# Conv-GLU layer on one core: eight Strassen pairs at distance two in the second half of the down projection, and a home of their own for the weights' sums

## What is computed

```python
def conv_glu_ffn(u, w_up, conv_ffn, b_conv_ffn, w_down):
    h = causal_dwconv(u @ w_up, conv_ffn) + b_conv_ffn
    return (jax.nn.silu(h[..., :D_FF]) * h[..., D_FF:]) @ w_down
...
        x = x + conv_glu_ffn(rms_norm(x, g_ffn[l]), w_up[l], conv_ffn[l], b_conv_ffn[l], w_down[l])
```

## Time and profile before

| | |
|---|---|
| time, median of 3 runs | 1744.62 us (1741.98 to 1744.79) |
| the profiled execution | 1744.25 us, its span 1742.5 us |
| busy: PE, DVE, ACT | 1732.3, 1184.1, 956.1 us (99, 68, 55%) |
| granted TensorE clock, mean | 0.999 |
| weights loaded by SP | 600 issues of 512 KB, median 3.3 us from issue to landing |

### The profile page before, as it was taken

One profiled execution on the slowest core, in us unless ns is written; L12 is line 12 of the kernel. 1 busy time (PEld: TensorE's weight loads), 2 busy tenths in 40 slices (PEclk: granted clock), 3 DMA queues, 4 the chain that ended last, 5 costly groups with the idle time before them and its releaser, 6 DMA issues.

```text
span 1742.5 us, 25685 instructions
## 1 busy us (share of the span) xinstructions
PE 1732.3 (99%) x8706; PEld 1470.0 (84%) x8706; DVE 1184.1 (68%) x1618; ACT 956.1 (55%) x1271; POOL 9.9 (1%) x22
## 2 busy tenths in 40 slices
PE   9999999999999999999999999999999999999999
PEld 7888888888788888888888888888888888888887
DVE  6788876667755455545565667777777666788777
ACT  7765656666754444444664565555555555555453
POOL 0000000000000000000000000000000000000000
PEclk9999999999999999999999999999999999999999
DMA  8555554476655555556855445555555555555654
GB/s 321 192 172 172 171 173 158 169 166 166 163 188 191 189 192 192 187 195 221 301 183 189 147 169 193 187 189 190 187 188 191 193 188 186 169 206 192 206 194 169
DMA packets 90960, 330.93 MB, mean 190 GB/s; under 512 B 10224, under 2 KB 10480, under 8 KB 89872
## 3 DMA queue, kind: packets, MB, share of 16 engines
q1 hardware_dynamic: 89424, 321.96, 54.7%
q0 software_dynamic: 1472, 8.12, 2.8%
HBM read 326.83 MB, written 2.10 MB: 189 GB/s over the span
## 4 chain that ended last, share of the span: by engine, by line
PE 93%; DVE 2%; DMA 2%; ACT 2%; issue 1%; SPq 0%; ACTq 0%; DVEq 0%
PE ps L381 22%; PE ps L362 13%; PE ps L364 13%; PE ps L363 13%; PE ps L384 11%; PE ps L756 4%; PE ps L758 4%; PE ps L757 4%; DMA w_raw<-in_stream 2%; PE ps L484 1%; PE ps L485 1%; PE ps L483 1%; PE ps L528 1%; PE ps L527 1%; ACT w_hi L843 1%
## 5 line engine op out<-in xcount | busy, mean ns | idle before, releaser
L1397 DVE TENSOR_TENSOR w_lo<-w_raw,w_hi 128x1024 fp32r<-128x1024 f32 x514 | 626.8, 1224 | 459.1 <-ACT w_hi L843 458.6
L843 ACT ACTIVATE w_hi<-w_raw 128x1024 fp32r<-128x1024 f32 x514 | 539.7, 1057 | 507.8 <-PE ps L364 309.7
L381 PE MATMUL ps<-u,w_hi 128*128 128x512 f32 x1664 | 580.8, 395 | 0.0
L384 PE MATMUL ps<-u,w_lo 128*128 128x256 f32 x1664 | 461.8, 278 | 0.0
L381 PEld LDWEIGHTS ps<-u,w_hi 128*128 128x128 f32 x1664 | 312.1, 188 | 72.4
L384 PEld LDWEIGHTS ps<-u,w_lo 128*128 128x128 f32 x1664 | 312.4, 188 | 0.2
L362 PE MATMUL ps<-w_hi,u 128*128 128x512 f32 x608 | 241.0, 396 | 0.6 <-DVE w_lo L1429 0.6
L364 PE MATMUL ps<-w_hi,u 128*128 128x512 f32 x608 | 237.4, 390 | 0.0
L363 PE MATMUL ps<-w_lo,u 128*128 128x512 f32 x608 | 237.0, 390 | 0.0
L362 PEld LDWEIGHTS ps<-w_hi,u 128*128 128x128 f32 x608 | 114.4, 188 | 24.6 <-issue 1.0
L364 PEld LDWEIGHTS ps<-w_hi,u 128*128 128x128 f32 x608 | 114.3, 188 | 24.2
(11 more groups left out here) (404 smaller groups left out, 2373.2 us busy)
## 6 DMA issues: line engine op xcount, KB each, us to landing
w_raw<-in_stream SPq DMA_DIRECT2D x600, 512.0 KB, 3.3
x_tok<-in_x SPq DMA_DIRECT2D x2, 1024.0 KB, 8.6
mem_raw<-in_mem_by_feature POOLq DMA_DIRECT2D x2, 1024.0 KB, 7.3
x_tok<-in_x POOLq DMA_DIRECT2D x2, 1024.0 KB, 7.6
mem_tok<-in_mem POOLq DMA_DIRECT2D x2, 1024.0 KB, 14.7
x_t<-in_x_t SPq DMA_DIRECT2D x7, 256.0 KB, 5.2
w_raw<-in_stream SPq DMA_DIRECT2D x4, 256.0 KB, 5.1
m_st<-ncm POOLq DMA_DIRECT2D x8, 128.0 KB, 9.4
```

Source lines behind the costliest of these rows:

```text
L381: pe.matmul(ps[:, bank + m, :], w_hi[:, s, lo:lo + P], act[:, kc, :, :].rearrange("p h t -> p (h t)"), start=(kc == 0), stop=False)
L384: mm = pe.matmul(ps[:, bank + m, T:2 * T], w_lo[:, s, lo:lo + P], act[:, kc, 0, :], start=False, stop=(kc == KC - 1))
L843: act.activation(w_hi[:, s, :], w_raw[:, s, :], ACT.Copy).then_inc(hi_made, 1)
L1397: TTo(w_lo[:, s, :], w_raw[:, s, :], w_hi[:, s, :].bitcast(F32), ALU.subtract).then_inc(lo_made, 1)
```

## The change

The second pass gets eight fast pairs at positions 4, 6, ..., 18, a distance of two; the first keeps its six. The activations' sums are made for eight pairs, in iterations 2 to 9 of the up projection. `u_sum` gets a place of its own, so that only `u_hi` and `u_lo` wait for `fast_done`. In the loop over n the staging comes ahead of the split and one pair earlier (n + 3); pair 2 is staged before the last iteration of the up projection, which is written out instead of looped. The last steps of iteration 10 are put after the splits of pairs 2, 3, 5 and 6. The space comes from the scratch of software DMAs, 4096 instead of the default.

```diff
-FAST_AT = (4, 7, 10, 13, 16, 19)
+FAST_AT = ((4, 7, 10, 13, 16, 19), (4, 6, 8, 10, 12, 14, 16, 18))
...
+ORDER = [_order(at) for at in FAST_AT]
+FAST = [(j, p, ORDER[j][p] // 2 - 1) for j in range(2) for p in FAST_AT[j]]
...
+        u_sum = sb("u_sum", [P, 4, BLK])
+        nr = region("n_rc", 4096, [("n_sum_c", [P, 2, BLK], F32)], [("n_lo_c", [P, 2, BLK], F32R)])
...
-            [("dpad", [P, 4096], F32), ("u_sum", [P, 4, BLK], F32), ("r_diag", [P, TT, P], F32),
+            [("dpad", [P, 4096 + 2048], F32), ("r_diag", [P, TT, P], F32),
...
-                begin, end = i == 0, i == len(FAST_AT) - 1
+                begin, end = p == FAST_AT[j][0], p == FAST_AT[j][-1]
...
-                pe.wait_ge(sem("u_low"), 2 * (len(FAST_AT) * j + i) + 2)
+                pe.wait_ge(sem("u_low"), 2 * done + 2)
...
-                    if p in FAST_AT:
+                    if p in FAST_AT[j]:
                         down_fast(j, p)
...
             def stage(p):
-                act.activation(h_high_pair(p), h_pair(h_ff, p), ACT.Copy).then_inc(sem("h_high"), 1)
+                q = ORDER[0][p]
+                act.wait_ge(sem("h_made"), q // 2 + 1 if p < 15 else UP_ITER)
+                act.activation(h_high(q), h_pair(h_ff, q), ACT.Copy).then_inc(sem("h_high"), 1)
...
-            with act.Fori(0, UP_ITER - 2 - len(FAST_AT)) as j:
-                up_pass(Pos(G_UP + (2 + len(FAST_AT)) * UP_PER, j, UP_PER), j + 2 + len(FAST_AT), False)
+            i_home = 2
+            with act.Fori(0, 2) as j:
+                up_pass(Pos(G_UP + 8 * UP_PER, j, UP_PER), j + 8, False, j + 6)
+            stage(2)
+            up_pass(Pos(G_UP + 10 * UP_PER), 10, False)
...
-                        if n == 2 and k == 0:
-                            up_first(UP_ITER - 1, 1, xb, ub)
...
             for n in range(2 * QN):
                 if n == 0:
                     up_low(UP_ITER - 1, 1, xb)
+                if n + 3 < QN:
+                    act.wait_ge(w_used, G_DOWN)
+                    stage(n + 3)
                 if n + 2 < 2 * QN:
                     down_split(n + 2)
-                if n + 2 < QN:
-                    act.wait_ge(w_used, G_DOWN)
-                    act.wait_ge(sem("h_made"), ORDER[n + 2] // 2 + 1 if n + 2 < 14 else UP_ITER)
-                    stage(n + 2)
-                if n % QN == FAST_AT[-1] + 1:
-                    act.wait_ge(sem("fast_done"), len(FAST_AT) * (n // QN + 1))
+                if n == 1:
+                    up_first(UP_ITER - 1, 1, xb, ub)
+                if n % QN == FAST_AT[n // QN][-1] + 1:
+                    act.wait_ge(sem("fast_done"), len(FAST_AT[0]) if n < QN else len(FAST))
...
                 for k in range(2):
                     dve.wait_ge(landed[s + k], Pos(g + k).landed(0))
-                if i:
-                    dve.wait_ge(sem("fast_done"), i)
                 if n >= QN:
                     dve.wait_ge(sem("half_sums"), 1)
...
                 dve.wait_ge(sem("u_sums"), 3 * i + 3)
+                if i:
+                    dve.wait_ge(sem("fast_done"), i)
                 for m in range(2):
...
+                if n + 3 < QN:
+                    stage(n + 3)
                 if n + 2 < 2 * QN:
                     down_split(n + 2)
-                if n + 2 < QN:
-                    stage(n + 2)
-                if n % QN == FAST_AT[-1] + 1:
+                if n == 0:
+                    up_scale(UP_ITER - 1, 1, xb)
+                if n == 3:
+                    up_tap(1, UP_ITER - 1, 1, xb, ub)
+                    up_tap(0, UP_ITER - 1, 1, xb, ub)
+                if n == 4:
+                    up_gate(UP_ITER - 1)
+                if n % QN == FAST_AT[n // QN][-1] + 1:
                     extra_sums(n // QN)
...
-    nc = bacc.Bacc("TRN2", target_bir_lowering=False, num_devices=1)
+    nc = bacc.Bacc("TRN2", target_bir_lowering=False, num_devices=1, dynamic_dma_scratch_size=4096)
```

More of the change, by code:

```diff
@@ L63, with _order @@
 QN = FC // 2
-FAST_AT = (4, 7, 10, 13, 16, 19)
-_fast = [2 * i for i in range(1, len(FAST_AT) + 1)]
-_plain = [q for q in range(QN) if q not in _fast]
-ORDER = [_fast.pop(0) if p in FAST_AT else _plain.pop(0) for p in range(QN)]
+FAST_AT = ((4, 7, 10, 13, 16, 19), (4, 6, 8, 10, 12, 14, 16, 18))
+FORMS = max(len(at) for at in FAST_AT)
+def _order(at):
+    fast = [2 * i for i in range(1, len(at) + 1)]
+    plain = [q for q in range(QN) if q not in fast]
+    return [fast.pop(0) if p in at else plain.pop(0) for p in range(QN)]
+ORDER = [_order(at) for at in FAST_AT]
+FAST = [(j, p, ORDER[j][p] // 2 - 1) for j in range(2) for p in FAST_AT[j]]
 G_END = G_DOWN + FC * 2
@@ L758, in three, with down_products @@
                 return pe.matmul(o, a_lo, b_hi, start=False, stop=last)
-            def down_products(s, p, k, t, n, bank, first=False, last=False):
+            def down_products(s, q, k, t, n, bank, first=False, last=False):
                 rows, at = slice(t * P, (t + 1) * P), slice(n * BLK, (n + 1) * BLK)
-                return three(ps[:, bank, :], h_high(p, k)[:, rows], h_lo[:, 2 * ORDER[p] + k, rows],
+                return three(ps[:, bank, :], h_high(q)[:, k, rows], h_lo[:, 2 * q + k, rows],
                              w_hi[:, s, at], w_lo[:, s, at], first, last)
@@ L771, in down_plain @@
                         for n in range(2):
[L772 to L773 removed]
+                            mm = down_products((g + k) % SLOTS, ORDER[j][p], k, t, n, 4 * j + 2 * t + n,
+                                               first=(p == 0 and k == 0), last=(j == 0 and p == QN - 1 and k == 1))
                     mm.then_inc(w_used, 1)
             def down_fast(j, p):
[L778 removed]
+                g, q = G_DOWN + 2 * (QN * j + p), ORDER[j][p]
+                i, done = q // 2 - 1, [(a, b) for a, b, c in FAST].index((j, p))
                 s0, s1 = g % SLOTS, (g + 1) % SLOTS
[L780 removed]
+                begin, end = p == FAST_AT[j][0], p == FAST_AT[j][-1]
                 c11, c12, c21 = (ps[:, 4 * j + b, :] for b in range(3))
@@ L796, in down_fast @@
                 pe.wait_ge(lo_made, g + 2)
-                three(e1, h_high(p, 0)[:, early], h_lo[:, k1, early], *weights(s0, right), begin, end).then_inc(w_used, 1)
-                three(c11, h_high(p, 1)[:, early], h_lo[:, k2, early], *weights(s1, left), False, False)
+                three(e1, h_high(q)[:, 0, early], h_lo[:, k1, early], *weights(s0, right), begin, end).then_inc(w_used, 1)
+                three(c11, h_high(q)[:, 1, early], h_lo[:, k2, early], *weights(s1, left), False, False)
                 pe.wait_ge(sem("n_low"), i + 1)
                 three(c12, *form(N3), *weights(s1, right), False, False).then_inc(w_used, 1)
-                pe.wait_ge(sem("u_low"), 2 * (len(FAST_AT) * j + i) + 2)
+                pe.wait_ge(sem("u_low"), 2 * done + 2)
                 three(e5, *form(N5), *sums(0), begin, end)
@@ L804, in down_fast @@
                 three(e6, *form(N6), *sums(2), begin, end)
-                three(c21, h_high(p, 1)[:, late], h_lo[:, k2, late], *sums(3), False, False).then_inc(sem("fast_done"), 1)
+                three(c21, h_high(q)[:, 1, late], h_lo[:, k2, late], *sums(3), False, False).then_inc(sem("fast_done"), 1)
             for j in range(2):
@@ L1991, in forms_low @@
                 dve.wait_ge(sem("n_high"), i + 1)
-                src, dst = ((n_sum_a[:, bass.ds(i, 1), :], n_lo_a[:, bass.ds(i, 1), :]) if i_home == 0 else
-                            (n_sum_b[:, bass.ds(i - 4, 1), :], n_lo_b[:, bass.ds(i - 4, 1), :]))
+                home, low, first = ((n_sum_a, n_lo_a, 0), (n_sum_b, n_lo_b, 4), (n_sum_c, n_lo_c, 6))[i_home]
+                src, dst = (a[:, bass.ds(i - first, 1), :] for a in (home, low))
                 TTo(dst, src, n_hi[:, bass.ds(i, 1), :].bitcast(F32), ALU.subtract).then_inc(sem("n_low"), 1)
             def stage(p):
+                q = ORDER[0][p]
                 dve.wait_ge(sem("h_high"), p + 1)
-                TTo(h_pair(h_lo, p), h_pair(h_ff, p), h_high_pair(p).bitcast(F32), ALU.subtract
-                    ).then_inc(sem("h_low"), 1)
+                TTo(h_pair(h_lo, q), h_pair(h_ff, q), h_high(q).bitcast(F32), ALU.subtract).then_inc(sem("h_low"), 1)
             up_pass(Pos(G_UP), 0, True)
@@ L2154, in lay_out @@
     for half in range(2):
-        for p, q in enumerate(ORDER):
+        for p, q in enumerate(ORDER[half]):
             pair = w_down[2 * q * P:(2 * q + 2) * P, 1024 * half:1024 * (half + 1)].reshape(2, P, 1024).copy()
-            if p in FAST_AT:
+            if p in FAST_AT[half]:
                 pair[0] = np.roll(pair[0], BLK, axis=1)
```

73 lines of the change are left out of this document (33 added, 40 removed).

## The result

The changed kernel takes 1755.28 us (median of 6 runs, 1752.83 to 1757.27) against 1744.26 us (6 runs) for the one before: a ratio of 1.0069, 95% interval 1.0058 to 1.0079. It is 11 us slower. The profiled execution took 1757.27 us, the longest of the six; its span is 1755.1 us.

The account below looks back on a forecast made before the run. PE, busy 1732.3 of 1742.5 us, was taken to bound the kernel. 1744.25 + 14.2 (second pass) - 1.6 (first pass) = 1756.9 us profiled, so 1757 us for the median, 0.7% slower; range 1750 to 1765 us.

Parts of the forecast that it names:

- the sum's 1756.9: Whole kernel: 1744.25 + 14.2 - 1.6 = 1756.9 us, against the profiled execution.
- The turn of the ring: Second pass: two slots reloaded in 5.6 us, then 7.0 us of split, 12.6 us against PE's 10.20 us of work.
- The second pass: Down projection's second pass: reloads at distance two stall PE before fast pairs, 129.8 us against 115.6, +14.2 us.
- 41.6 + 7c: Second pass's length: first split at +20.50 us, seven turns of c, then 4.76 + 16.32 us of PE's work.
- The first pass: Down projection's first pass: staging ahead of the split removes stalls for staged activations; it ends 1.6 us earlier.
- the stalls came as laid out: First pass: no wait for `h_lo`, but PE stalls of 0.85 and 1.9 us before the first two fast pairs.
- the lower bound of 0: First pass: no gain if the new stall of 1.9 us drops PE's clock, costing 1.5 us.
- The clock: Second pass: a stall each turn may drop PE's clock; 1.5 us more makes 11.7, still under 12.6, absorbed in the stall.
- the private place of `u_sum`: Second pass: claimed no help, since `fast_done` comes 4.8 us after a fast pair starts and sums can't begin before 5.6.
- a quicker reload: Second pass: both slots reloaded in 4.6 us, turn 11.6 us, pass +7.2 us, time 1750 us; chance 12%.
- The clock's own turn of 13.8 us: Second pass: 18 matmuls per turn at 1.2 GHz make PE's work the bound, pass +22.6 us, time 1765 us; chance 10%.

Follow-up runs that it names:

- work off and on the ring: Changed kernel plus two unused VectorE instructions per turn of the second pass: behind plain pairs' splits 1754.89 us, inside fast pairs' splits before the slots are freed 1764.51 us.
- half the bytes: Changed kernel with each load of the second pass bringing only half a chunk, these loads written out instead of looped: 1743.27 us, ratio 1.0002.
- the slots freed earlier: Changed kernel with the fast pair's split reordered, `w_hi` ahead of `u_hi` and `w_lo` ahead of `u_lo`: 1736.45 us, ratio 0.9966 to the kernel before.
- the run with distance three: Changed kernel with six fast pairs at distance three in the second pass too, old split order: 1743.02 us, ratio 1.000 to the kernel before.
- the experiment with the wait first: Changed kernel with VectorE's wait for `fast_done` put back ahead of the weights' sums: 1763.55 us, ratio 1.0118 to the kernel before.

## Why the prediction was right, point by point

- **The time.** 1757 us was forecast, 1755.28 measured, within 1750 to 1765. The forecast difference was 12.4 us, the measured one 11.0. That the profiled execution, at 1757.27 us, comes so close to the sum's 1756.9 is in part luck: it was the longest of the six, and 0.8 us that the first pass gained less than forecast were made up by 0.9 us from elsewhere (below).
- **The turn of the ring**, c = 12.6 us from a reload of 5.6 and a split of 7.0: measured 12.62, 5.6 and 7.0. The reload could be read before the change because ScalarE had been idle and waiting for the very same pair of loads, where it cost PE nothing. The experiments with work off and on the ring, with half the bytes and with the slots freed earlier show that it is this chain, and neither VectorE's load nor the number of instructions. The reload was 5.13 to 6.41 us long, so 5.6 is right as a mean only; VectorE's idle time before the sums was 1.2 to 4.1 us where 2 to 3 was forecast.
- **The second pass**: +14.2 us forecast (41.6 + 7c = 129.8). The pass took 129.9 us where 115.6 was reckoned for before; from the pass's start to the end of the span it is 133.8 us against 119.5, +14.3.
- **The first pass**: 1.6 us forecast, 0.8 measured, 1.6 in the run with distance three. No wait for `h_lo` is left, and the stalls came as laid out, 0.95 and 2.22 us for 0.85 and 1.9. Behind the second, eight matmuls ran slow in the changed kernel's profile (1.5 us) and none in the run with distance three (stall 2.23 us); that was the lower bound of 0, which is partly met. Some 0.9 us came from elsewhere, since the down projection began at 1501.02 us instead of 1501.87; in the profiles of the experiments it begins between 1500.97 and 1502.28, so that is scatter.
- **The clock** fell behind three of the stalls in the changed kernel's profile (one of them in the first pass) and not behind the others. In the second pass it was absorbed in the turn, as the sum had it (11.7 us of PE's work under 12.6): behind the two slow fast pairs the turns to the next freeing took 12.15 and 12.88 us, behind the others 12.49 to 13.42. In the one experiment where `fast_done` stood on the chain it was not absorbed. The prediction expected a slow clock behind the stalls more often than it came.
- **What I had wrong**: that the private place of `u_sum` doesn't help. The step compared 4.8 us (`fast_done`, at the full clock) with 5.6 (reload). Even at the full clock that was too tight: in the experiment with the wait first the pair behind 1655.16 ends 4.9 us after its start, and where PE released the sums they began another 0.36 us later, 5.25 us in all, which is longer than two of the seven reloads (5.13 and 5.15 us). And I had the low clock as likely in the same paragraph: 4.76 + 1.8 us and the latency are 6.9. The two terms stood side by side and were not put together. The forecast was right because the change had moved the wait.
- **The rivals**: a quicker reload, 4.6 us, didn't occur (5.13 us is the shortest of seven). The clock's own turn of 13.8 us (18 slow matmuls) didn't occur in the changed kernel, whose longest turn, 13.42 us, has the longest reload in it. The turn of 13.95 us in the experiment with the wait first is close to it by coincidence: there 7 or 8 matmuls were slow, and the turn is 6.9 us to the sums and 7.0 us of split.

## What to carry to other kernels

When work is packed closer in a ring of buffers, first reckon the ring's own turn: from the freeing of a slot over its reload to the next freeing. The trace of the old kernel may hold both pieces, as here, in waits that cost nothing yet. Then free the slot as early as the data allow: the same computing instructions in another order turned a change that lost 11 us into one that gains 7. VectorE's busy share did not tell whether one more instruction costs here, its place in the chain did.

## What was not expected of the hardware

How long a stall was did not tell whether the clock fell behind it. Windows of the changed kernel, each from the end of a stall of 2.22, 2.38 and 3.34 us:

```profile
1541.40:1545.00 3.60, 3.60 (x9) 2.86 (x10) 3.33 (x4) 1.33 (x3) 0.00 (x0) 0.55 0.69 246
1691.40:1695.00 3.60, 3.60 (x10) 2.86 (x11) 2.15 (x2) 0.00 (x0) 0.00 (x0) 0.57 0.67 237
1717.60:1721.00 3.40, 3.37 (x15) 2.80 (x16) 2.25 (x2) 0.01 (x1) 0.00 (x0) 1.00 0.68 230
```

and of the kernel with distance three, behind a stall of 2.23 us at the place of the first of these:

```profile
1542.30:1546.00 3.70, 3.68 (x16) 3.07 (x17) 3.35 (x4) 1.42 (x3) 0.00 (x0) 1.00 0.71 249
```

The granted clock is 0.55 and 0.57 behind the first two and 1.00 behind the longest; behind the fourth, as long as the first, it is 1.00 as well. Over the down projections of all ten profiles there are 24 stalls of 2.22 us or more; slow matmuls came behind 16 of them, 6 to 8 each time. Behind the shorter ones, the longest of 2.16 us, there were none. So the price of a stall of 2.2 us or more is here its length plus either nothing or some 1.5 to 1.8 us, and what decides between the two these traces don't show.
